# Attention of the second block: transpositions two items behind the scores, with three pairs of exponential buffers

## What is computed

```python
def diff_attend(q, k, v, lam):
    s = jnp.einsum('bhmqd,bhmkd->bhmqk', q, k).astype(jnp.float32) * (QK_DIM ** -0.5)
    p = jax.nn.softmax(s, axis=-1)
    p = p[:, :, 0] - lam * p[:, :, 1]
    return jnp.einsum('bhqk,bhkd->bhqd', p.astype(v.dtype), v)
```

## Time and profile before

| | us |
|---|---|
| median of 3 runs | 3701.85 |
| lowest and highest | 3697.41, 3704.54 |
| time of the profiled execution | 3698.28 |
| span in its profile | 3696.5 |
| TensorE busy (matmuls), share of the span | 3464.0, 94% |
| VectorE busy | 2522.1, 68% |
| ScalarE busy | 1900.7, 51% |
| GpSimd busy | 840.6, 23% |

### The profile page before, as it was taken

The page is one execution under the profiler, slowest core; times in us unless marked ns, Lnnn a source line. Parts: engine busy times, 40 slices in busy tenths (PEclk is TensorE's granted clock), DMA queues, the critical chain, the costliest instruction groups (busy, mean ns, idle before and its releaser), DMA issues. The chain is left out here.

```text
span 3696.5 us, 43311 instructions
## 1 busy us (share of the span) xinstructions
PE 3464.0 (94%) x16712; PEld 2810.4 (76%) x16712; DVE 2522.1 (68%) x2823; ACT 1900.7 (51%) x2500; POOL 840.6 (23%) x665
## 2 busy tenths in 40 slices
PE   7999988968879999999999998999899889998989
PEld 4887844668758888888888877788788677887867
DVE  6545268789568889889889886565686555416763
ACT  6211132476627777777777765441575233515750
POOL 2100036411211112121121114200343233103432
PEclk9999999988989999999999999999999999999999
DMA  5554225221548999999999985365411542625123
GB/s 210 201 191 159 92 84 205 71 111 43 189 166 352 387 392 380 389 380 386 393 380 387 393 301 177 114 210 177 148 58 54 187 129 83 181 98 174 51 95 120
DMA packets 325799, 766.70 MB, mean 207 GB/s; under 512 B 29400, under 2 KB 119123, under 8 KB 325592
## 3 DMA queue, kind: packets, MB, share of 16 engines
q1 hardware_dynamic: 303482, 689.48, 50.6%
q0 software_dynamic: 17184, 63.97, 5.3%
q10 hardware_dynamic: 4928, 10.49, 0.8%
HBM read 652.38 MB, written 111.48 MB: 207 GB/s over the span
## 5 line engine op out<-in xcount | busy, mean ns | idle before, releaser
L3686 DVE TENSOR_TENSOR first_expert_w_low<-shared_z,first_expert_w_high 128x2048 fp32r<-128x2048 f32 x127 | 295.1, 2356 | 59.7 <-ACT first_expert_w_high L3637 59.2
L3686 DVE TENSOR_TENSOR moe_w_low<-moe_w_raw,moe_w_high 128x2048 fp32r<-128x2048 f32 x128 | 287.5, 2287 | 38.3 <-ACT moe_w_high L3637 38.3
L3686 DVE TENSOR_TENSOR moe_w_low<-shared_z,moe_w_high 128x2048 fp32r<-128x2048 f32 x128 | 288.2, 2287 | 22.4 <-ACT moe_w_high L3637 22.2
L3927 POOL TENSOR_SCALAR layer_att_p<-layer_att_p,layer_att_rinv,layer_att_neg_lam 128x1280 f32<-128x1280 f32 x72 | 173.3, 2409 | 512.9 <-DVE layer_att_neg_lam L3959 315.0
L3637 ACT ACTIVATE first_expert_w_high<-shared_z 128x2048 fp32r<-128x2048 f32 x126 | 237.3, 1923 | 69.0 <-PE moe_bank L182 49.1
L3637 ACT ACTIVATE moe_w_high<-shared_z 128x2048 fp32r<-128x2048 f32 x128 | 240.2, 1923 | 49.0 <-PE moe_bank L182 40.2
L3637 ACT ACTIVATE moe_w_high<-moe_w_raw 128x2048 fp32r<-128x2048 f32 x128 | 238.8, 1919 | 30.8 <-PE moe_bank L182 28.7
L182 PE MATMUL moe_bank<-moe_w_high,first_expert_xgT_low 128*128 128x512 f32 x640 | 249.0, 389 | 0.0
L180 PE MATMUL moe_bank<-moe_w_high,first_expert_xgT_high 128*128 128x512 f32 x640 | 249.0, 389 | 0.0
L181 PE MATMUL moe_bank<-moe_w_low,first_expert_xgT_high 128*128 128x512 f32 x640 | 249.0, 389 | 0.0
L3936 DVE TENSOR_REDUCE layer_att_nb<-layer_att_scores 128x1 f32<-128x1280 f32 (+1 forms) x144 | 193.9, 1368 | 75.2 <-PE layer_att_scores L3834 73.8
(11 more groups left out here) (722 smaller groups left out, 9422.4 us busy)
## 6 DMA issues: line engine op xcount, KB each, us to landing
shared_z<-in_exp_w SPq DMA_DIRECT2D x256, 1024.0 KB, 10.1
moe_w_raw<-in_exp_w SPq DMA_DIRECT2D x128, 1024.0 KB, 8.8
shared_z<-in_w_in SPq DMA_DIRECT2D x48, 512.0 KB, 6.1
first_raw<-in_w_in SPq DMA_DIRECT2D x32, 512.0 KB, 7.5
front_vec<-in_ada_w POOLq DMA_DIRECT2D x16, 1024.0 KB, 6.0
proj_t<-front_out SPq DMA_DIRECT2D x48, 256.0 KB, 2.0
shared_z<-in_w_mod SPq DMA_DIRECT2D x24, 512.0 KB, 4.4
k_high<-layer_front_staged SPq DMA_DIRECT2D x20, 512.0 KB
```

Source lines behind the costliest of these rows:

```text
L3686: nc.vector.tensor_tensor(lo, x, hi.bitcast(F32), ALU.subtract).then_inc(low, 1)
L3927: last = nc.gpsimd.tensor_scalar(b, b, rinv[:, j, 1:2], neg_lam[:, :], ALU.mult, ALU.mult)
```

## The change

```diff
-    LAG, PAIR, RIDES = 3, 2, 2
+    LAG, PAIR, RIDES = 2, 2, 2
```

## The result

The changed kernel takes 4027.49 us (median of 4 runs, 4026.72 to 4032.79) against 3700.34 (4 runs, 3697.41 to 3704.54) for the kernel before. The ratio is 1.088, with a 95% interval of 1.087 to 1.0895: slower by 327 us. The forecast was 4037, in a range of 3905 to 4085. The profiled execution took 4026.72 us with a span of 4024.8, and the one of before a span of 3696.5, so there are 328.3 us to explain between the two traces.

The account below looks back on a forecast made before the run. TensorE was taken to bound the kernel (152.6 of 155 us busy). 208 + 4 + 123 = 335 us on the profiled 3698.3 gave 4033, and 3.6 us up to the median gave 4037; range 3905 to 4085.

Parts of the forecast that it names:

- The mechanism: Attention stages: TensorE waits behind score(i, 0) for VectorE's mix(i-2), delaying all queued work; 3.46 us mean per step.
- The pauses: Attention stages: 60 TensorE waits for the mix, 30 in each layer, of 3.46 us mean: 208 us.
- the riders: Layer 0: longer bounds and mixes add 1.0 us for each of 8 items; between 0 and 8 us, taken as 4.
- The clock: Attention stages: nearly each pause brings 4.1 us of TensorE work at 1.2 GHz, losing 2.05 us per step: 123 us.
- The shorter list: End of each layer's attention: one step fewer, its work moving into the other steps; costed at nothing.
- The buffers: Attention stages: the third pair fewer costs nothing, being free once item i-3 is transposed.
- GpSimd: Attention stages: its product of item i-2, 2.63 us, is released a step before the mix and costs nothing.
- score(i+1, 0) on its exponentials: Attention stages: exps(i, 0) comes later, 2.8 us after the pause, but TensorE's 4.3 us of own work covers it.
- Outside the stages: Rest of the program, outside both attention stages: nothing should change.
- Full clock, 3914: Rival, attention stages: the clock stays at 2.4 GHz and only the pauses count; 3914 us, chance 0.13.
- A clock that hardly recovers: Rival, attention stages: every burst runs at the lower level throughout, 5.6 us more per step; 4250 us, chance 0.04.
- Faster: Rival, attention stages: no wait, and each layer loses one step of 5.0 us; 3692 us, 10 less, chance 0.02.

Follow-up runs that it names:

- the kernel with both layers filled: Changed kernel with 26 unread matmuls of 256 columns between score(i, 0) and the transpositions, in both layers: 3909.55 us.
- the values first: Changed kernel with the value products of a step moved ahead of the first transpositions on TensorE: 3863.54 us.
- the early copy: Kernel before, with VectorE's copy of finished values moved from the next step's start to behind the same step's mix: 3693.02 us against 3699.23.

## Why the prediction was right, step by step

**The mechanism.** TensorE asks for item i-2 behind score(i, 0), VectorE has it only after the bounds and the mix, and all that is queued behind the wait moves with it. The row of waits (62 times, ended by the mix) and the timeline show just this. Two experiments pin it to the order of the two lists: putting the mix late in the kernel before makes the same loss, and putting it first in the changed kernel takes more than half of it away.

**The pauses: 208 + 4 us predicted.** 209 measured, by the kernel with both layers filled, and 202.3 by the growth of idle time. The sum holds, but its parts only because small misses cancel. In the timeline of after each layer has 31 pauses, not 30: the 31st stands in the first step without scores, 4.47 us in layer 0 and 4.46 in layer 1, in the drain that I had costed at nothing. The other 60 make 218.4 - 8.9 = 209.5 us, 100.5 in layer 1 and 109.0 in layer 0.

In layer 1, where 30 x 3.46 = 104 was forecast, a step costs a little less. The transpositions start 3.58 us behind the last score matmul (3712.76 to 3716.34) where they started 0.13 behind it (3436.05 to 3436.18): 3.45 us later, and 3.57 was forecast for a step without a copy. Most of that miss is the handoff, which takes 0.05 us (the mix ends at 3716.29), not the 0.15 that I took from a copy. The profile gives 3.30 us of idle time for this pause, as it counts from the modelled end of the last score matmul. The other value, 3.45, stands in every second step, in which VectorE's copy of finished values comes ahead of the bound of map 0.

In layer 0 the riders add 8.5 us and not 4. The longest pauses, up to 4.56 us, stand where the first of two rider items is mixed: the bound and the mix are longer there, and the reciprocal waits another 0.21 us for ScalarE's exponentials of the rider, a wait that I had left out. In three of the four cases the step before has 3.91. About 3.8 us stand where VectorE also copies a rider's values.

**The clock: 123 us predicted.** 118 measured by filling the pauses, 126 by the growth of TensorE's busy time. The lower level was taken to last 4.1 us of work in each step, so that 2.05 us are lost; 126 / 60 gives 2.1. That it came so near was in part luck: three stretches of 3.4, 3.75 and 6.6 us stood behind the 4.1, and the slow groups of value products in after take anything from 3.24 to 4.47 us. That it falls at nearly every pause was the step with the most room in it, and the row of 29 slow groups of value products bears it out.

The Trainium skill, "TensorE: Matmul & The Clock Gate", section "Why this matters for your kernels", warns of pauses above about 3 us. The pauses of 3.3 us and more fit that. But the clock also fell behind pauses of 2.01 us with the mix first, and in steps whose pauses were shorter still with the values first. By the page's figure those steps would have lost nothing, where 31.5 and 57.8 us more work was measured in the two kernels.

**What was costed at nothing.** The shorter list: wrong by the two waits in the drain above. The buffers: 4024.7 us with four pairs, no difference that one run could tell. GpSimd: its product takes 2.63 us as before and ends no wait of TensorE; VectorE's last mix of each layer waits for it, 2.6 us in both together against 1.6 before. score(i+1, 0) on its exponentials: 7.1 us in 4 waits, less than before. Outside the stages: 528.5 us between them against 526.8.

**The rivals.** Full clock, 3914: the filled kernel makes that case real, at 3909.55, so the price was right, and the granted clock of 0.80 says that it didn't occur. A clock that hardly recovers: the scores after the pause's burst are back at 0.49 us, so no. Faster: would have needed the mix to be done before the transposition.

**Where expectations missed.** Four: the late mix has two pauses fewer; the kernel with the mix first came 1 us under its range; the clock's cost with the values first was put near nothing and is 58 us, so that the time came out between the two cases that were named; and the early copy gave the program 6 us instead of 13. The third is the one to learn from, since I read "shorter than any pause that did harm so far" as "harmless".

## What to carry to other kernels

A software pipeline's lag is to be counted in the lists of both engines: take from the trace when the producer finishes, and where the consumer asks. Here VectorE finished item i-2 in the middle of step i, so a consumer that asks at the start of step i+1 waits for nothing, one that asks at the start of step i waits for most of VectorE's step, and all that it has queued waits with it.

TensorE's pause in each step had two prices here, its length and the work that then ran at the lower clock, and the second was more than half as large as the first. Where the pause stayed, shortening it by 1.6 us gave back 94 us of clock beside 106 of waiting, and unread matmuls in it gave back some 59 us a layer, though they add work. Neither comes near to giving the consumer its step of distance.

## What the runs showed of the hardware that I had not expected

**GpSimd's product depends on VectorE's neighbour.** The same 128x1280 multiplication on GpSimd, in the kernel before and in the one with the mix first (ns, shortest/median/longest; the first row is that of before):

```profile
L3927 POOL TENSOR_SCALAR layer_att_p<-layer_att_p,layer_att_rinv,layer_att_neg_lam x72: 546/2640/2960, 2616.4 to 3530.9; 128x1280 f32<-128x1280 f32 x64, 128x256 f32<-128x256 f32 x8
...
L3927 POOL TENSOR_SCALAR layer_att_p<-layer_att_p,layer_att_rinv,layer_att_neg_lam x72: 550/1407/1419, 2618.6 to 3664.1; 128x1280 f32<-128x1280 f32 x64, 128x256 f32<-128x256 f32 x8
```

It takes 2.64 us where it starts with VectorE's mix, as in the earlier trace rows, and 1.41 where the mix is over before it starts, 1.9 times as fast; VectorE's mix takes 1.53 us beside it and 1.54 alone (medians). All of GpSimd's work in the program falls from 840.6 to 760.9 us. The Trainium skill, "GPSIMD Engine Reference", section "Key points", tells of SBUF interfaces shared with VectorE and of contention with its instructions that have two SBUF inputs; the mix has two, and the runs agree. That GpSimd alone pays is what they show in this case. But for the last mix of each layer nobody waits for GpSimd here, so it costs next to nothing.

**Short pauses and the clock.** With two pauses in each step, of 0.95 and 0.75 us in the steps shown, TensorE's granted clock was 0.91 to 0.93 over a stage; with one of 1.88 us it was 0.92 to 0.96; with one of 3.5 us 0.80. So the cost is not nothing at 2 us, and it doesn't follow the length of a single pause: the two short ones added 57.8 us of work, the one of 1.88 us 31.5. What does decide stays open.
